# A hybrid SSD + HGRN2 + PEER block on one Trainium2 core: the sequence goes through the mixers in two token halves, and all dense gates are scattered instead of built from one-hot products

## The chip, the cores and the metric

The kernel runs on one core of one Trainium2 chip. The metric is device time in microseconds (us) of that core. A core has five engines that run their own instruction streams: TensorE (PE in the rows, with its weight loads as PEld), VectorE (DVE), ScalarE (ACT), GpSimd (POOL) and SyncE (SP), which only issues transfers here. Everything is in fp32.

## The reference

One encoder block on 1024 tokens of width 1024:

```python
hn   = rmsnorm(x, ln_mix_w)
z, xbc, dt_raw, q, f, i, g = split(hn @ w_in)          # 7184 columns
y_ssd = ssd_mixer(z, xbc, dt_raw, ...)                 # Mamba-2: 16 heads in 4 groups, state 128
y_hg  = hgrn2_mixer(q, f, i, g, lb, hg_norm_w)         # 8 heads, keys and values 128
h = x + concat(y_ssd, y_hg) @ w_out
xn = rmsnorm(h, ln_ffn_w)                              # PEER: 8 product-key heads
s  = (xn @ w_query) . sub_keys                         # 2 x 128 scores per head and token
expert, gate = top 16 of the 16 x 16 best pairs, softmax
y  = sum_k gelu(xn . u_table[expert_k]) * gate_k * v_table[expert_k]
out = rmsnorm(h + y, ln_final_w)                       # 16384 experts, 128 picks per token
```

Both mixers are recurrences over the sequence: the state after one chunk of tokens enters the next.

## The kernel before, in words

Tokens are cut into 8 blocks (chunks) of 128; a half is 4 of them. The program is a row of stages, each in a block of its own, at whose end every engine waits for all others.

1. `input_norm` normalises and turns x.
2. `ssd` goes over 4 groups, and in each over both halves. PE projects ("pieces") the next group-half while it runs the 4 chunks of this one; the first group-half is projected ahead of the first chunk. POOL makes one `ssd_awide` for each chunk. The last 8 chunks carry the pieces of HGRN2's head 0.
3. `hgrn` goes over 8 heads of 8 chunks. 56 chunks carry the pieces of the next head, the last 8 ("deep") have none. On DVE, `attend` forms each chunk's attention: seven strided products of the level scores with a mask (L1057), one more (L1059), and a sum over the levels (L1063). ACT starts two transfers that zero the part of the table `sel` that belongs to one pair of blocks.
4. `mix_out` multiplies by w_out, adds x, normalises (block by block), and runs 16 of the 32 query and score steps. A step gives the scores of two units; a unit is one head for one block of 128 tokens. DVE routes 32 of the 64 units here: MAX8, FIND_INDEX8 and MATCH_REPLACE8 of both key lists (L1176 to L1189), 54 candidate pairs, `route_hit` (L1219, L1221), its sum (L1223), indices and gate. POOL first scales Y (L1595), then scatters the gates of block 0 into `sel` in DRAM: 8 units of 16 indirect transfers each (L1604).
5. `peer`: blocks 0 to 3 are dense (every expert's row is multiplied, and the gates are read from `sel`); blocks 4 to 7 are gathered (the rows of the picked experts are fetched). For dense blocks 1 to 3 the gate table is first built: DVE makes one-hot rows (L2156, L2160), PE multiplies them (L1939), ACT copies them out and they are stored to `sel`. 96 such rounds stand ahead of the main loop.
6. The main loop goes over 16 groups of 8 first-keys: PE forms u products (L1958) and then v products (L1971), 256 slots in all, with 13 query steps (L1888, L1903) between. POOL gathers 512 rows of u and 512 of v, each of 128x1024; DVE multiplies and adds them (L2185, L2196), and routes the last 31 units.

The order on each engine is written out by hand in the code; semaphores join the engines.

Of the kernel before, what the change touches and what calls it, by code (L numbers as in the profile page):

```python
# [9 lines left out]
U32 = mybir.dt.uint32  # L10

P = 128
SEQ, D = 1024, 1024
NB = SEQ // P
KT = D // P
# [7 lines left out]
TAPS = 4  # L23
SSD_COLS = CT * P + XW + HPG
# [11 lines left out]
HEAD_PARTS = [[0], [1], [2, 3], [4, 5]]  # L36
LEVELS = 7
# [10 lines left out]
DB = NB // 2  # L48
DU, GU = PH * DB, PH * (NB - DB)
UNITS = DU + GU  # L50
DS, STEPS = DU // 2, UNITS // 2
GE = 8
NG = KEYS // GE
SLOTS = 2 * GE
UT = 3
PAIRS = GU * TOPK // 2
ROWS = GU * TOPK
# [4 lines left out]
MB = DB - 1  # L62
PAIR = 2 * DB * P
# [8 lines left out]
class Own:  # L72
# [17 lines left out]
    def skip(self):  # L90
        self.eng.sem_inc(self.sem, 1)
        self.n += 1

# [12 lines left out]

def prime(eng, sems):
    for s in sems:
        eng.sem_inc(s, 1)


def constants(nc, pool, C, filled, cut, ident_ready):
# [10 lines left out]
    nc.gpsimd.memset(C["lmask"][:], 1.0).then_inc(filled, 1)  # L123
# [11 lines left out]
                            base=0, pattern=[[0, NB], [1, P]], channel_multiplier=0)  # L135
    n = 0
    for j in range(LEVELS):
# [3 lines left out]
        m = C["lmask"][:, j, :].rearrange("p (q two r) -> p q two r", two=2, r=h)  # L141
# [9 lines left out]
    nc.gpsimd.affine_select(out=C["lmask"][:, LEVELS, :], in_=C["lmask"][:, LEVELS, :],  # L151
                            compare_op=ALU.is_equal, fill=0.0,
                            base=0, pattern=[[-1, P]], channel_multiplier=1).then_inc(cut, 1)
    pool.wait_ge(cut, n + 1)


def input_norm(nc, x, ln_w, w_ssd, C, hnT, w_group, group_in):


    with ExitStack() as ctx:  # L160
# [12 lines left out]

        xs = sb("xs", [P, NB, D])
# [16 lines left out]
        def _(sp):  # L191
# [5 lines left out]
            for i, part in enumerate(SSD_PARTS):  # L197
                sp.dma_start(w_group[:, :, part], w_ssd[0, :, :, part]).then_inc(group_in[i], 16)

        @block.gpsimd  # L200
        def _(pool):
            constants(nc, pool, C, filled, cut, ident_ready)
# [46 lines left out]
def first_weights(Y, kt):  # L249

    return Y[:, kt // 2, D + kt % 2 * HG_COLS:D + (kt % 2 + 1) * HG_COLS]


def first_piece(Y, half, p):

    if p < 2:
        return Y[:, KT // 2 + p, D + half * HALF:D + (half + 1) * HALF]
    return Y[:, KT // 2 + 2 + half, D + (p - 2) * 2 * P:D + (p - 1) * 2 * P]


def first_raw(Y, half):

    vg = Y[:, KT // 2 + 2 + half, D:MIX].rearrange("p (c x) -> p c x", x=2 * P)
    return first_piece(Y, half, 0), first_piece(Y, half, 1), vg[:, :, P:2 * P], vg[:, :, 0:P]


class Heads:
# [3 lines left out]
    def __init__(self, nc, ctx, first, hw):  # L271
# [12 lines left out]
        flat = first.rearrange("p k c -> p (k c)")  # L284
        self.first = flat
        self.w = hw[:, 0:KT * HG_COLS].rearrange("p (k c) -> p k c", k=KT)
# [3 lines left out]
        self.v = [sb("v0", [P, HC, P])]  # L290
        self.gs = [sb("gs0", [P, HC, P])]
        self.gend = sb("gend", [P, NB])
        self.G, self.k, self.q, self.ke, self.qs = [[flat[:, i * HALF:(i + 1) * HALF]] for i in range(5)]
        self.W = [flat[:, 5 * HALF:(5 + LEVELS) * HALF].rearrange("p (j l) -> p j l", j=LEVELS)]
        self.w_in, self.lb_in = [plain_sem(f"w_in{i}") for i in range(len(HG_PARTS))], plain_sem("lb_in")
        self.lb_diff, self.lb_ready = sem("lb_diff"), sem("lb_ready")
# [6 lines left out]
    def second(self, nc, ctx):  # L303
        def sb(name, shape):
            return ctx.enter_context(nc.sbuf_tensor("head_" + name, shape, F32))
# [11 lines left out]
def heads_act(nc, act, H, n, half, part, raw):  # L317

    raw_q, raw_f, raw_g = raw
    G, W = H.G[half], H.W[half]  # L320
    if part == 0:
        nc.scalar.activation(G, raw_f, ACT.Sigmoid).then_inc(H.gate_sig, 1)
        nc.scalar.activation(H.q[half], raw_q, ACT.Silu).then_inc(H.q_ready, 1)
# [15 lines left out]
def heads_dve(nc, dve, prep, H, u, half, part, reset, raw_v):  # L339
# [41 lines left out]
    else:  # L381
# [4 lines left out]
        prep.check()  # L386


def ssd(nc, w, w_in, w_ssd, par, w_hg, lb_logits, C, hnT, Y, spent, hw, H):

# [1955 lines left out]
```

## Time and profile before

| | |
|---|---|
| median of 3 runs | 3615.16 us (3612.87 to 3615.65) |
| span of the profiled execution | 3610.9 us, 4.3 under the median |
| PE busy | 3447.2 us, 95% of the span |
| DVE busy | 2815.0 us, 78% |
| POOL busy | 1422.8 us, 39% |
| ACT busy | 1079.8 us, 30% |
| granted TensorE clock, mean | 0.981 of full speed |

The profiled execution has no time of its own apart from its span, which counts from the first to the last instruction; what lies around the span is taken as the 4.3 us between it and the median. A high busy share says that the engine has work in most of the span. It doesn't say which engine ends a given stage.

### The profile page before, as it was taken

How to read it: one execution, taken by the hardware profiler on the slowest of the kernel's cores; microseconds unless marked ns; L12 is line 12 of the kernel's file. 1: busy time of each engine (PE TensorE's matmuls, PEld its weight loads, DVE VectorE, ACT ScalarE, POOL GpSimd, SP SyncE). 2: the span in 40 equal slices, each digit the busy share in tenths (PEclk: the TensorE clock that was granted, in tenths of full speed). 3: DMA queues.
4: the chain of work that ended last, by engine and by line, in shares of the span. 5: the costliest groups of instructions: out<-in, count | busy, mean ns of one | idle time of the engine just before them, and what ended most of it. 6: DMA issues, size and time to landing. Idle time of an engine off the chain costs nothing.

```text
span 3610.9 us, 39997 instructions
## 1 busy us (share of the span) xinstructions
PE 3447.2 (95%) x11593; PEld 1976.1 (55%) x11593; DVE 2815.0 (78%) x6484; ACT 1079.8 (30%) x2721; POOL 1422.8 (39%) x1233
## 2 busy tenths in 40 slices
PE   7999999999997999768799999999999999999998
PEld 4666666777774566556344444444444444444443
DVE  2466686776774389899788888987898889888898
ACT  3233344544442222268221112111211121121212
POOL 1000000000001277500566565655666566655665
PEclk9999999999997999989899999999999999999999
DMA  3111013000002234247999999999999999999998
GB/s 112 30 36 35 0 32 109 23 23 29 29 35 114 50 60 91 34 139 203 394 393 377 393 380 392 379 380 356 394 372 387 386 397 377 375 394 377 390 376 340
DMA packets 313936, 829.65 MB, mean 230 GB/s; under 512 B 41504, under 2 KB 145056, under 8 KB 305056
## 3 DMA queue, kind: packets, MB, share of 16 engines
q0 software_dynamic: 165888, 537.01, 39.9%
q1 hardware_dynamic: 125104, 227.45, 17.4%
q10 hardware_dynamic: 22768, 63.18, 4.5%
q8 instruction: 69, 1.13, 0.1%
q14 instruction: 107, 0.88, 0.1%
HBM read 789.73 MB, written 37.81 MB: 229 GB/s over the span
## 4 chain that ended last, share of the span: by engine, by line
PE 46%; issue 5%; DVE 3%; DMA 2%; POOL 1%; ACT 0%; ACTq 0%; DVEq 0%; POOLq 0%
PE peer_ps_o L1971 23%; PE peer_ps_d L1958 20%; PE peer_ps_q L1888 2%; DMA peer_vr<-in_v_rows,peer_index 2%; DVE Y L2196 1%; POOL peer_vr L1863 0%; DVE peer_mt L2156 0%; DVE peer_mt L2160 0%; POOL peer_ur L1856 0%; DVE peer_ur L2185 0%; PE peer_ps_s L1903 0%; DMA peer_ur<-in_u_rows,peer_index 0%; DVE route_hit L1221 0%; DVE peer_chosen L1223 0%; DVE Y L2213 0%
## 5 line engine op out<-in xcount | busy, mean ns | idle before, releaser
L1856 POOL DMA_INDIRECT peer_ur<-in_u_rows,peer_index x512 | 566.1, 1106 | 600.1 <-DVE peer_ur L2185 418.7
L2196 DVE SCALAR_TENSOR_TENSOR Y<-peer_vr,osq,Y 128x1024 f32<-128x1024 f32 x512 | 656.7, 1283 | 100.2 <-DMA peer_vr<-in_v_rows,peer_index 99.8
L1863 POOL DMA_INDIRECT peer_vr<-in_v_rows,peer_index x512 | 588.3, 1149 | 324.9 <-issue 148.2
L2185 DVE SCALAR_TENSOR_TENSOR peer_ur<-peer_ur,Y 128x1024 f32<-128x1024 f32 x512 | 627.6, 1226 | 8.0 <-DMA peer_ur<-in_u_rows,peer_index 8.0
L1958 PE MATMUL peer_ps_d<-hnT,route_ut 128*128 128x512 f32 x1376 | 598.6, 592 | 0.7 <-ACT peer_vr L2031 0.7
L1971 PE MATMUL peer_ps_o<-hw,Y 128*128 128x512 f32 x1024 | 446.2, 595 | 14.8 <-DVE Y L2172 14.7
L1971 PE MATMUL peer_ps_o<-hnT,Y 128*128 128x512 f32 x1024 | 442.6, 592 | 0.0
L1958 PEld LDWEIGHTS peer_ps_d<-hnT,route_ut 128*128 128x128 f32 x1376 | 261.2, 190 | 328.6 <-issue 327.7
L1971 PEld LDWEIGHTS peer_ps_o<-hw,Y 128*128 128x128 f32 x1024 | 194.9, 191 | 257.5 <-issue 235.9
L1971 PEld LDWEIGHTS peer_ps_o<-hnT,Y 128*128 128x128 f32 x1024 | 193.5, 190 | 238.2 <-issue 238.0
L1958 PE MATMUL peer_ps_d<-hnT,peer_ut 128*128 128x512 f32 x672 | 297.3, 595 | 6.7 <-ACT Y L2039 6.7
L2046 ACT ACTIVATE osq<-osq 128x2 f32<-128x2 f32 x256 | 51.2, 200 | 786.5 <-DVE peer_ur L2185 786.4
L2039 ACT ACTIVATE Y<-peer_ps_d 128x512 f32<-128x512 f32 x128 | 76.4, 597 | 672.9 <-PE peer_ps_d L1958 672.9
L1604 POOL DMA_INDIRECT sel<-route_ut,mo_sel_index x128 | 208.2, 1626 | 151.0 <-DVE route_ut L1247 83.1
L512 PE MATMUL ssd_ps_piece<-hnT,w_group 128*128 128x512 f32 x512 | 229.8, 602 | 6.9 <-ACT hw L595 5.1
L1589 POOL IOTA mo_count_u<- 128x128 uint32 x1 | 0.2, 239 | 590.6 <-POOLq L816 590.6
L1958 PEld LDWEIGHTS peer_ps_d<-hnT,peer_ut 128*128 128x128 f32 x672 | 128.2, 191 | 168.0 <-issue 168.0
L494 POOL TENSOR_TENSOR ssd_awide<-ssd_a,tri 128x512 f32<-128x512 f32 x32 | 34.5, 1078 | 453.3 <-PE ssd_ps_rows L556 404.5
L905 PE MATMUL hg_ps_piece<-hnT,hw 128*128 128x512 f32 x448 | 198.7, 597 | 4.3 <-ACTq L1027 4.3
L909 PE MATMUL hg_ps_piece<-hw,hnT 128*128 128x256 f32 x896 | 198.0, 379 | 0.0
L909 PEld LDWEIGHTS hg_ps_piece<-hw,hnT 128*128 128x128 f32 x896 | 168.1, 190 | 21.7
L512 PEld LDWEIGHTS ssd_ps_piece<-hnT,w_group 128*128 128x128 f32 x512 | 98.8, 193 | 129.6 <-issue 123.7
(331 smaller groups left out, 5018.8 us busy)
## 6 DMA issues: line engine op xcount, KB each, us to landing
route_ut<-in_u_cols SPq DMA_DIRECT2D x86, 512.0 KB, 7.4
hw<-in_v_cols SPq DMA_DIRECT2D x16, 2048.0 KB, 11.0
peer_mt<-sel ACTq DMA_DIRECT2D x64, 512.0 KB, 9.2
hnT<-in_v_cols SPq DMA_DIRECT2D x16, 2048.0 KB, 13.6
peer_ut<-in_u_cols SPq DMA_DIRECT2D x42, 512.0 KB, 7.3
route_wk<-in_w_route ACTq DMA_DIRECT2D x14, 1024.0 KB, 7.8
hnT<-in_w_route SPq DMA_DIRECT2D x9, 1024.0 KB, 4.8
route_wk<-in_w_route SPq DMA_DIRECT2D x9, 1024.0 KB, 6.9
```

Of the source, the lines that this page charges most:

```text
L512: mm = nc.tensor.matmul(bank, w[:, k, i * P:(i + 1) * P], hnT[:, half, k, :], start=(k == 0), stop=(k == KT - 1))
L905: mm = nc.tensor.matmul(bank, w[:, kt, p * P:(p + 1) * P], hnT[:, half, kt, :], start=(kt == 0), stop=(kt == KT - 1))
L909: mm = nc.tensor.matmul(bank[:, 0:2 * P], hnT[:, half, kt, cols(p - 2)], w[:, kt, 2 * P:4 * P], start=(kt == 0), stop=(kt == KT - 1))
L1604: pool.indirect_dma_start(sel.rearrange("a i q two (t o) -> (a i q two t) o", o=1), bass.IndirectOffsetOnAxis(ap=sel_index[:, h, k:k + 1], ...
L1856: pool.indirect_dma_start(ur[:, r % RING, :], None, u_rows, bass.IndirectOffsetOnAxis(ap=index[:, r // TOPK % 4, r % TOPK:r % TOPK + 1], a ...
L1863: pool.indirect_dma_start(vr[:, r % RING, :], None, v_rows, bass.IndirectOffsetOnAxis(ap=index[:, r // TOPK % 4, r % TOPK:r % TOPK + 1], a ...
L1888: mm = nc.tensor.matmul(ps_q[:, p, :], wq[:, k, p * P:(p + 1) * P], xg[:, k, :], start=(k == 0), stop=(k == KT - 1))
L1958: mm = nc.tensor.matmul(ps_d[:, e % 2, :], ut[e % UT][:, k, :], xT[:, k, :], start=(k == 0), stop=(k == KT - 1))
L1971: mm = nc.tensor.matmul(ps_o[:, o % OB, :], ht(e, tb), v_tile(e, half), start=(j == 0), stop=(j == GE - 1))
L2039: nc.scalar.activation(ht(e), ps_d[:, e % 2, :], ACT.Gelu).then_inc(gelu_done, 1)
L2185: nc.vector.scalar_tensor_tensor(out=ur[:, s, :], in0=ur[:, s, :], scalar=1.0, in1=Y[:, b, D:MIX], op0=ALU.mult, op1=ALU.mult, accum_out=d ...
L2196: nc.vector.scalar_tensor_tensor(out=hb, in0=vr[:, s, :], scalar=hid[:, c:c + 1], in1=hb, op0=ALU.mult, op1=ALU.add).then_inc(comb_done, 1)
```

## The change

The three stages ssd, hgrn and mix_out now run for tokens 0 to 511 and then again for tokens 512 to 1023; peer follows. SSD states, HGRN2 states (`held`) and the convolution's last columns (`carry`) are kept in SBUF between the halves. The weights of the mixers and w_out are loaded once in each half. Each half does two heads' first pieces in its ssd stage (`EARLY_HEADS`), so a half's hgrn stage has 24 chunks with pieces and 8 without.

All 32 dense units (`DENSE`) have their gates scattered to `sel`, 512 scatters in place of 128. The one-hot rounds, with their products, copies and stores, are gone. `sel` is zeroed as a whole (32 MB in 16 transfers, one for each chunk of the first ssd stage). Units 0 to 21 are routed in the first mix_out, 22 to 27 at the start of the second ssd stage, 28 to 31 within its first 8 chunks, 32 to 43 in the second mix_out, 44 to 63 in peer, which has 10 query steps in its loop. `attend` is now eight predicated copies, each after the one before (the next waits for it), with no sum; the mask is one of bytes.

```diff
+EARLY_HEADS = 2
+ROUTED_IN = [range(0, 22), range(UNITS // 2, 2 * ROUTED_STEPS)]
+ROUTE_BEFORE, ROUTE_AFTER, ROUTE_CHUNKS = range(22, 26), range(26, 28), range(28, 32)
+SCATTER_MIX0, SCATTER_PROLOGUE, SCATTER_SSD = DENSE[0:6], DENSE[6:9], DENSE[9:14]
+SCATTER_CHUNK = 5
+SCATTER_HG, SCATTER_MIX1 = DENSE[14:25], DENSE[25:]
...
+def scatter(nc, pool, R, sel, n, ks):
+    b, h, at = unit_block(n), unit_head(n), DENSE.index(n)
+    for k in ks:
+        if k == 0:
+            pool.wait_ge(R.routed, n + 1)
+            pool.wait_ge(R.gated, n + 1)
+            need(pool, R.scattered[b], 16 * TOPK * h)
+        nc.gpsimd.indirect_dma_start(sel..., IndirectOffsetOnAxis(ap=R.index_d[:, at, k:k + 1], axis=0),
+                                     R.gates_d[:, at, k:k + 1], None,
+                                     compute_op=ALU.add).then_inc(R.scattered[b], 16)
...
# ssd, GpSimd
+                for n in SCATTER_PROLOGUE:
+                    scatter(nc, pool, R, sel, n, range(TOPK))
...
                     nc.gpsimd.tensor_tensor(awide[:], ...)
+                    if half == 1:
+                        at = (t - first * HC) * SCATTER_CHUNK
+                        for q in range(at, min(at + SCATTER_CHUNK, len(SCATTER_SSD) * TOPK)):
+                            scatter(nc, pool, R, sel, SCATTER_SSD[q // TOPK], range(q % TOPK, q % TOPK + 1))
...
# hgrn, GpSimd
+            if half == 1:
+                for n in SCATTER_HG:
+                    scatter(nc, pool, R, sel, n, range(TOPK))
...
# hgrn, VectorE
-                    nc.vector.tensor_tensor(right(masked[:]), bank[:, j, 0:P // 2].rearrange(...),
-                                            right(C["lmask"][:]), ALU.mult)
-                nc.vector.tensor_tensor(masked[:, LEVELS, :], bank[:, LEVELS, :], C["lmask"][:, LEVELS, :],
-                                        ALU.mult).then_inc(mask_done, 1)
-                dve.wait_ge(mask_done, past(u * NB + c + 1))
-                nc.vector.tensor_reduce((att2 if lag and c % 2 else att)[:], masked[:].rearrange("p j l -> p l j"), AX.X,
-                                        ALU.add).then_inc(att_ready, 1)
+                    nc.vector.copy_predicated(right(to[:]), right(C["lmask"][:, j, :]),
+                                              bank[:, j, 0:P // 2].rearrange(...)).then_inc(G.placed, 1)
+                    dve.wait_ge(G.placed, past(t * LEVELS + j + 1))
+                nc.vector.copy_predicated(to[:], C["lmask"][:, LEVELS, :], bank[:, LEVELS, :]).then_inc(G.att_ready, 1)
...
# mix_out, GpSimd
-            for h in range(PH):
-                pool.wait_ge(R.routed, 2 * h + 1)
-                for k in range(TOPK):
-                    pool.indirect_dma_start(...).then_inc(R.scattered, 16)
+            for n in (SCATTER_MIX0, SCATTER_MIX1)[half]:
+                scatter(nc, pool, R, sel, n, range(TOPK))
...
# peer, VectorE and TensorE: the rounds ahead of the main loop
-                nc.vector.tensor_tensor(hot_a[j % 2], R.count[:]..., pickedT[:, b % 2, 0, t:t + 4]..., ALU.is_equal)
-                    ins = nc.vector.tensor_scalar(hot_b[j % 2][:, q, :], R.count[:], ..., ALU.is_equal, ALU.mult)
-                    mm = nc.tensor.matmul(ps_o[:, j % 2, q * P:(q + 1) * P], hot_a[j % 2][:, q, :], hot_b[j % 2][:, q, :])
```

**POOL.** Before, GpSimd has one awide for each of 32 chunks, nothing from there to mix_out but a memset, and its 128 scatters in mix_out (`Y<-Y,osq` is the scaling; `peer_ur` and `peer_vr` are the first gathers of the main loop):

```order
L494 TENSOR_TENSOR ssd_awide<-ssd_a,tri 128x512
L892 MEMSET hg_zero 128x256
L1595 TENSOR_TENSOR Y<-Y,osq 128x1024 x8
L1604 DMA sel<-route_ut,mo_sel_index 8388608x1 x128
L1856 DMA peer_ur<-in_u_rows,peer_index 128x1024 x5
L1863 DMA peer_vr<-in_v_rows,peer_index 128x1024 x5
```

In the changed kernel, from the first mix_out to the start of peer, the same engine has this:

```order
L1403 DMA sel<-lists 8388608x1 x96
L1403 DMA sel<-lists 8388608x1 x48
L559 TENSOR_TENSOR ssd_awide<-ssd_a,tri 128x512
L1403 DMA sel<-lists 8388608x1 x5
...
L1403 DMA sel<-lists 8388608x1 x176
L1770 TENSOR_TENSOR Y<-Y,osq 128x1024 x4
L1403 DMA sel<-lists 8388608x1 x112
L1969 DMA peer_ur<-in_u_rows,index_g 128x1024 x5
L1977 DMA peer_vr<-in_v_rows,index_g 128x1024 x5
```

96 scatters stand in the first mix_out, 48 ahead of the second ssd stage's first awide, 5 behind each of its 16 awides, 176 in the second hgrn stage, which had no GpSimd work before, and 112 in the second mix_out, ahead of all gathers.

**DVE, attend.** Before, VectorE has for each HGRN2 chunk (first rows of the stage's body):

```order
L1057 TENSOR_TENSOR hg_masked<-hg_ps_att,lmask 128x64
L1057 TENSOR_TENSOR hg_masked<-hg_ps_att,lmask 128x2x32
L1057 TENSOR_TENSOR hg_masked<-hg_ps_att,lmask 128x4x16
...
L1059 TENSOR_TENSOR hg_masked<-hg_ps_att,lmask 128x128
L1063 TENSOR_REDUCE hg_att<-hg_masked 128x128
```

and in the changed kernel:

```order
L1162 COPY_PREDICATED hg_att<-lmask,hg_ps_att 128x64
L1162 COPY_PREDICATED hg_att<-lmask,hg_ps_att 128x2x32
L1162 COPY_PREDICATED hg_att<-lmask,hg_ps_att 128x4x16
...
L1166 COPY_PREDICATED hg_att<-lmask,hg_ps_att 128x128
L404 TENSOR_SCALAR head_G<-head_G,head_oml,head_lb 128x512
```

Eight instructions stand for nine, and the copies write the attention tile itself.

**DVE, a chunk of the second ssd stage.** In each of its first 8 chunks half a unit's routing now stands between the preparation of the next group (`ssd_step`) and the update of the state, which before followed it directly:

```order
L788 TENSOR_SCALAR ssd_step<-ssd_step 128x16
L1315 MAX route_ti<-Y 128x8 x2
L1318 MAX_INDEX route_ix<-route_ti,Y 128x8
...
L1353 MAX route_best<-route_cand 128x8
L1355 MAX_INDEX route_place<-route_best,route_cand 128x8
L896 TENSOR_TENSOR state<-state,ssd_decay_all 128x256
```

## Rows read from the trace of the kernel before

**Rows 1.** Windows: length, busy us of each engine, PEclk, DMA share, GB/s.

```profile
28.20:121.70 93.50, 88.40 (x261) 50.66 (x261) 13.16 (x26) 15.63 (x28) 1.14 (x2) 0.95 0.15 46
121.70:446.90 325.20, 325.20 (x1235) 208.44 (x1235) 214.68 (x507) 121.80 (x202) 24.96 (x24) 1.00 0.08 23
446.90:538.90 92.00, 84.23 (x365) 59.47 (x364) 75.19 (x184) 39.42 (x66) 8.75 (x8) 0.99 0.08 24
538.90:1129.90 591.00, 564.14 (x2816) 430.59 (x2816) 437.37 (x1243) 268.10 (x570) 0.44 (x3) 0.96 0.12 39
1129.90:1219.60 89.70, 83.34 (x254) 43.70 (x255) 7.99 (x17) 18.93 (x61) 14.87 (x8) 0.96 0.32 128
1219.60:1547.00 327.40, 297.00 (x1115) 193.93 (x1113) 275.84 (x1140) 85.16 (x247) 208.17 (x128) 0.96 0.32 61
1547.00:1703.50 156.50, 125.82 (x849) 107.63 (x850) 147.66 (x429) 135.13 (x395) 5.25 (x5) 0.96 0.60 177
1703.50:3611.00 1907.50, 1868.72 (x4640) 872.10 (x4640) 1636.90 (x2930) 374.11 (x1117) 1149.10 (x1019) 0.99 0.98 381
```

**Rows 2.** Timeline of PE, ssd: start, us, line, [idle before].

```profile
135.31 0.38 PE L553 MATMUL ssd_ps_cb<-ssd_xc 128*128 128x128 f32 x2
...
148.85 0.38 PE L553 MATMUL ssd_ps_cb<-ssd_xc 128*128 128x128 f32 x2
```

**Rows 3.** Timeline of PE, hgrn: its start and two chunks.

```profile
547.17 8.81 PE L905 MATMUL hg_ps_piece<-hnT,hw 128*128 128x512 f32 x16 [4.30 <-ACTq L1027]
...
565.91 1.68 PE L926 MATMUL hg_ps_att<-w_group 128*128 128x64 f32 x14
...
575.39 1.67 PE L926 MATMUL hg_ps_att<-w_group 128*128 128x64 f32 x14
```

**Rows 4.** Timeline of DVE, one attend in hgrn.

```profile
1078.63 1.01 DVE L1057 TENSOR_TENSOR hg_masked<-hg_ps_att,lmask 128x64 f32<-128x64 f32 x7 [0.70 <-PE hg_ps_turn L928]
...
1079.87 1.92 DVE L1063 TENSOR_REDUCE hg_att<-hg_masked 128x128 f32<-128x1024 f32 x1
```

**Rows 5.** Groups of POOL: busy, mean ns, idle before by releaser.

```profile
L1863 POOL DMA_INDIRECT peer_vr<-in_v_rows,peer_index x512 | 588.3, 1149 | 324.9 <-issue 148.2 <-DMA sel<-peer_vr 117.2 <-DVE Y L2196 59.6
...
L1604 POOL DMA_INDIRECT sel<-route_ut,mo_sel_index x128 | 208.2, 1626 | 151.0 <-DVE route_ut L1247 83.1 <-issue 45.9 <-DMA sel<-route_ut,mo_sel_index 22.0
...
L1595 POOL TENSOR_TENSOR Y<-Y,osq 128x1024 f32<-128x1024 f32 x8 | 14.9, 1897 | 7.4 <-DVE osq L1644 7.4
...
L1589 POOL IOTA mo_count_u<- 128x128 uint32 x1 | 0.2, 239 | 590.6 <-POOLq L816 590.6
```

**Rows 6.** The scatters by source: ns min/median/max, first and last start.

```profile
L1604 POOL DMA_INDIRECT sel<-route_ut,mo_sel_index x128: 1542/1543/2417, 1234.9 to 1509.4; - x128
```

**Rows 7.** Timeline of POOL, two scatters in a row.

```profile
1240.73 1.54 POOL L1604 DMA_INDIRECT sel<-route_ut,mo_sel_index  x1 [0.30 <-issue]
...
1242.58 1.54 POOL L1604 DMA_INDIRECT sel<-route_ut,mo_sel_index  x1 [0.30 <-issue]
```

**Rows 8.** Timeline of DVE, mix_out: block 2's h, then units.

```profile
1245.70 1.22 DVE L1659 TENSOR_TENSOR Y<-mo_ps_h,hnT 128x1024 f32<-128x1024 f32 x1 [6.53 <-PE mo_ps_h L1405]
...
1251.63 0.48 DVE L1176 MAX8 route_ti<-route_sc 128x8 f32<-128x128 f32 x2
...
1260.99 0.48 DVE L1176 MAX8 route_ti<-route_sc 128x8 f32<-128x128 f32 x2
```

**Rows 9.** The chain that ended last, peer: start, us, engine, tile.

```profile
1786.75 23.13 PE peer_ps_o L1971 x50
...
1838.24 54.93 PE peer_ps_d L1958 x128
...
2363.84 6.91 PE peer_ps_q L1888 x32
...
2489.24 6.91 PE peer_ps_q L1888 x32
```

**Rows 10.** DMA issues of the span to 1140: KB, us to landing.

```profile
w_group<-in_w_ssd SPq DMA_DIRECT2D x16, 512.0 KB, 4.1
```

More of the change, by code:

```diff
@@ new lines, in _ @@
+            for n in (first, first + 1):
+                for p in range(SSD_PIECES):
+                    piece(n, p)
+            sums(first)
+            for n in range(first, end):
+                for c in range(HC):
+                    t, at = n * HC + c, cols(spot(n, c))
+                    if c == 0:
+                        pe.wait_ge(S.activated, past((n + 1) * CT))
+                    pe.wait_ge(S.wide_ready, past(t + 1))
+                    pe.wait_ge(S.att_ready, past(t))
+                    nc.tensor.matmul(ps_cb[:, 0:P], xc[:, 2, at], xc[:, 3, at], start=True, stop=True)
@@ new lines, in _ @@
+            if half == 1:
+                for i in range(2):
+                    sp.dma_start(ut[i], u_cols[i]).then_inc(R.u_in[i], 16)
+            load_x(first + 2)
+            load_queries(step + 2)
+            load_keys(step + 2)
+            load_queries(step + 3)
+            load_x(first + 3)
+            load_keys(step + 3)
+            loads(step + 4)
+            key_loads(step + 4)
+            loads(step + 5)
+            key_loads(step + 5)
+            for i in TAIL:
+                load_queries(i)
+                load_keys(i)
@@ L1523, in root @@
             def root(b):
-                act.wait_ge(h_meaned, past(b + 1))
-                nc.scalar.activation(rs[:, b:b + 1], ss[:, b:b + 1], ACT.Sqrt).then_inc(h_rooted, 1)
-            for b in range(NB):
-                now, late = HEADS_IN[b], late_head(b - 1)
-                if b == FIRST:
+                act.wait_ge(M.h_meaned, past(b + 1))
+                nc.scalar.activation(rs[:, b:b + 1], ss[:, b:b + 1], ACT.Sqrt).then_inc(M.h_rooted, 1)
+            unit = 2 * step
+            out_y(first, EARLY)
@@ L1542, in _ @@
                     out_y(b + 1, LATE)
-                    query_out(now[2])
-                    gates(2 * now[1])
+                    query_out(step + 2)
+                    gates(unit + 2)
                     continue
-                if late is not None:
-                    score_out(late)
-                    gates(2 * late - 1)
-                if b == NB - 1:
-                    for g in range(DB, DB + 2):
-                        x_copy(g, 0)
-                        x_copy(g, 1)
@@ L1584, in _ @@
-            gates(DU - 1)
-            score_out(DS)
+                if at == HC - 1:
+                    score_out(step + 3)
+                    query_out(step + 4)
+                    gates(unit + 6)
+                root(b)
+                if at == HC - 1:
+                    gates(unit + 7)
+                    score_out(step + 4)
+                    query_out(step + 5)
+            done = unit + 8
+            for i in TAIL:
+                if i == PH:
+                    x_copy(end - 1, 0)
+                    x_copy(end - 1, 1)
+                query_out(i)
+                score_out(i - 1)
+                if i > TAIL[0]:
+                    gates(done)
+                    done += 1
@@ L1685, in peer @@
+                if at == FIRST:
+                    for n in range(unit + 2, unit + 6):
+                        route(n)
+            routed = unit + len(ROUTED_IN[half])
+            for n in range(unit + 8, routed):
+                route(n)
+            for n in range(routed - GATE_LAG, routed):
+                route_gates(nc, dve, R, n)
+def peer(nc, w_route, u_cols, v_cols, u_rows, v_rows, fin_w, sel, C, Y, osq, hw, hnT, R, ut, out):
     with ExitStack() as ctx:
@@ L2291, in laid_out @@
+        peer(nc, w_route, u_cols, v_cols, u_rows, v_rows, fin_w, sel, C, Y, osq, hw, hnT, R, ut, out)
 def laid_out(inputs):
```

1981 lines of the change are left out of this document (953 added, 1028 removed).

## Prediction

> **What bounds the kernel now.** I read first where time goes by stage. A window for each stage [rows 1] gives 93.5 us (first projection of ssd), 325.2 (24 ssd chunks with pieces), 92.0 (the last 8), 591.0 (hgrn), 89.7 and 327.4 (mix_out up to and from the first routed unit), 156.5 (the one-hot rounds) and 1907.5 (the main loop). In each the reader should set PE's busy time against the length: 325.2 of 325.2, 564 of 591, 1869 of 1908, but only 297 of 327.4 in the routed part of mix_out (DVE 275.8) and 126 of 156.5 in the rounds (DVE 147.7). So PE bounds ssd, hgrn and peer; mix_out and the rounds are shared with DVE.
>
> Then the period of each repeated piece. An ssd chunk with pieces takes 148.85 − 135.31 = 13.54 us [rows 2], an hgrn chunk with pieces 575.39 − 565.91 = 9.47 [rows 3]. In peer's chain, the query steps at 1893.17 (1838.24 + 54.93) and 2363.84 are four groups apart, 117.67 each; a group without a query step has 110.7 (6.91 less) [rows 9].
>
> Last the engine that the change loads, POOL. It idles 590.6 us until the end of hgrn [rows 5]: nothing crosses a stage's end, so its scatters can't run ahead into another stage. A scatter takes at least 1.54 us of POOL [rows 6], and two undisturbed ones start 1.85 apart [rows 7]. Over all 128 the busy time is 208.2 and the issue gaps 45.9, 1.985 each, and 22.0 went into landing waits [rows 5].
>
> **The price of a unit of scatters.** Floor 16 × 1.85 = 29.5 us; the mean of before 16 × 1.985 = 31.8; with the landing waits 34.5 ((208.2 + 45.9 + 22.0)/8). The landing wait is for the head before of the same block; the changed order alternates two blocks, so a whole unit lies between, and I drop it. The long scatters of before (up to 2.42 us [rows 6]) fall in stretches of routing on DVE. In the second hgrn stage DVE does no routing, so I take 30.8, between floor and mean.
>
> The Trainium skill, "SBUF — State Buffer", section "Who interferes with whom", says that copies, casts and tensor_scalar on VectorE can hold a port pair that GpSimd needs to write descriptors, while tensor_tensor and tensor_reduce don't hold descriptor writing up. The spread of 1.54 to 2.42 us agrees, but doesn't single out which instruction did it. By that rule the hgrn stage, with few such instructions, would run near the floor, 29.5 a unit, and the whole sum below would come out 14 us lower for the 11 units of that stage.
>
> **The sum by stages**, from the span's 28.2 us where input_norm ends.
>
> *First ssd half.* 93.5 + 8 chunks with ssd pieces (8 × 13.54 = 108.3) + 92 = 293.8: ends at 322. The zeroing of 32 MB adds 2 MB a chunk, 5.5 us of 13.54 at peer's 381 GB/s, where the DMA share is 0.08 [rows 1]: hidden; if it is not, weights come late by some us a group.
>
> *First hgrn half.* Of the 56 chunks with pieces it has 24, and all of the last 8: 591 − 32 × 9.47 = 288. The start's 4.3 us wait [rows 3] goes, since the second head's pieces are made ahead; 1.5 for the stage's end. attend took 1.24 for its eight products and 1.92 for the sum [rows 4], 3.2. Eight predicated copies cost at least 1.2 (no dearer than the products), and, each waiting for the one before, at most 8 × 0.48 = 3.8 (a short dependent DVE step, MAX8's row [rows 8], is the nearest). I take 2.6. It counts only in the 8 chunks without pieces, elsewhere PE's 9.47 covers it: −4, ends −16 to +5. So 281 (269 to 290): ends at 603.
>
> *First mix_out half.* 89.7 to the first unit; then 22 units on DVE. A unit is 1260.99 − 1251.63 = 9.36 [rows 8], with its gate 9.7: 213.6. Blocks 2 and 3's h stand between: 6.53 idle and 5.93 from h to the next unit [rows 8] for the first, some 19 for both. 322.5; the 6 scattered units (185 us) fit beside. Ends at 925.5. DVE sets this stage: PE has about half of mix_out's 380 us.
>
> *Second ssd half.* 293.8 again, plus: the first weights are loaded inside the stage, 4.1 us [rows 10], I take 4.5; the gates of 4 units and their waits ahead of the first chunk, 4; three units (48 scatters, 92 us) ahead of the first awide are just done when it is wanted, 3. Four units' routing (39 us) goes into the first 8 chunks. DVE idles (325.2 − 214.7)/24 = 4.6 us a chunk, 37 in eight [rows 1], but in pieces, and half a unit is 5.5 in one chunk and 3.8 in the next: between 8 and 20 us late, I take 13. Five scatters a chunk (9.6) fit in 13.54. 318.5: ends at 1244.
>
> *Second hgrn half.* PE's path is 281 as before. POOL has 11 units: 11 × 30.8 = 339 (325 to 350). It starts them at the stage's start, the last lands before no one may leave: 340.5, ends near 1584. This is the term that decides: 59 us of waiting for POOL.
>
> *Second mix_out half.* DVE: 89.7 + 12 × 9.7 + 15 = 221. POOL scales 4 blocks (7.4 idle, then 4 × 1.86 [rows 1, 5]: 14.9), then 7 units, 215.6: 230 and 1.5 for the end. POOL ends it too: 1815.5, which I round down to 1814.5, since its start waits are partly DVE's.
>
> *peer.* No rounds, no stores to `sel` that v gathers wait for (117.2 us of POOL's waits [rows 5], before the loop's steady part). From the first u product to the first v product it took 1786.75 − 1703.50 = 83.3 [rows 1, 9]. Now there is a query step as well (6.9) and no store: at least 54.9 + 6.9 = 62, at most 90; I take 73, for the first u rows and routes must still come. Then 55.8 (2 × 27.47 + 0.89, the chain's 1838.24 − 1786.75 is 51.5 for what was left of it), 15 groups, 9 of them with a query step: 9 × 117.67 + 6 × 110.76 = 1723.6. The end: 3610.9 less 1838.24 less 13 × 117.67, 2 × 110.76 and the one long group's 7.7 (2363.84 to 2489.24 is 125.4) leaves 13.8. 1866, against 1907.5. Ends at 3681.
>
> With the 4.3 us between the span and the median: **3685 us**, +1.9%. Against before by parts: ssd +102, hgrn −29, mix_out +127, rounds −156.5, peer −41, together +2; POOL's hold +59 and +9. The DVE routing that filled time in mix_out beside 8 blocks' products now has only half of them to hide behind, and that eats the rounds' gain; POOL then decides the sign.
>
> **The rivals.**
>
> *Scatters at their floor and cheap attends.* 11 × 29.5 = 325 and 7 × 29.5 = 206.5: −14 and −9; attends at 1.2 take another 10 in the first hgrn half. 3652, up to 3668. For it: two scatters in a row show 1.85 [rows 7]. Chance 0.2.
>
> *Dearer scatters.* At 34.5 a unit (each waits for a landing, or DVE disturbs it) hgrn has 380 and mix_out 242 + 15: +40 and +26. With the ssd stage's routing at its upper end, 3715 to 3755. For it: the rate of before, taken whole. Against: the order of blocks. Chance 0.12.
>
> *POOL is off the path (no change).* Were the scatters to overlap, or an hgrn stage as long as POOL's by another cause, the sum without POOL's hold is 3617, against 3615.2. It needs a unit under 281/11 = 25.5 us, 1.6 us a scatter, which would have to be less than busy time and gap together show (1.85). Chance 0.07.
>
> *Faster.* POOL's hold must be gone (as above), or the rest must be 75 us better: mix_out's first half is the place. If DVE's units there don't wait for the start of 89.7 and take 1 us less each than I reckon (22 us), and peer starts in 62 rather than 73, and the copies are at 1.2, the sum falls by 22 + 11 + 12 = 45 and POOL's hold grows by nothing: 3640, still slower. It decides only with scatters below 27 us a unit as well (11 × 3.8 = 42 less): 3600. Chance 0.1.
>
> **How the numbers follow.** Forecast (POOL holds the second hgrn and mix_out stages, 3668 to 3715) 0.51, floor 0.2, dearer 0.12, no change 0.07, faster 0.1. The range leaves out the faster and no-change cases and the upper part of the dearer one, and reaches down into the floor case: 3640 to 3725. A measurement of this kernel can tell about 0.2% (7 us) from no change. Faster 0.1, same 0.07, slower 0.83.
>
> **What would show it.** In the second hgrn stage PE would have some 60 us idle at the end, with POOL's 176 scatters end to end at 1.92 us; the stage 340 us against 281 of the first. In the first mix_out DVE near 90% busy from its first unit to its end, PE about 60%. In the second ssd stage chunks of 14 to 16 us in the first eight and 13.5 in the first half's. In peer the period stays 117.67 and its length is about 1866. It would be wrong if scatters run under 27 us a unit, if chunks of hgrn stay PE-bound but take longer (copies dearer than 3.8), if the routing in ssd costs more than 20 us, or if peer's gathers, now free of the stores, shorten its groups below PE's 110.7, which PE's work rules out.

## The result

The changed kernel takes 3754.69 us (median of 4 runs, 3748.37 to 3756.04) against 3615.35 us: a ratio of 1.0386, 95% interval 1.0371 to 1.0400. It is slower by 139 us. The forecast was 3685 with a range up to 3725; the sign was right, the size was not.

The span of the profiled execution is 3754.3 us. PE is busy 3378 us of it (90%, before 95%), DVE 2654 (71%), POOL 2062 (55%, before 39%). The windows of the changed kernel by stage, in the columns of [rows 1]: first ssd, first hgrn, first mix_out, second ssd, second hgrn until PE's last product, from there to the stage's end, second mix_out, peer.

```profile
28.20:314.70 286.50, 278.12 (x1024) 177.34 (x1024) 155.11 (x373) 96.69 (x163) 18.90 (x19) 0.99 0.45 161
314.70:597.20 282.50, 259.62 (x1312) 200.31 (x1312) 184.60 (x595) 126.75 (x268) 0.02 (x1) 0.94 0.18 58
597.20:926.00 328.80, 253.58 (x992) 174.16 (x992) 210.16 (x907) 62.52 (x188) 165.26 (x102) 0.88 0.35 85
926.00:1230.50 304.50, 283.90 (x1024) 180.94 (x1024) 249.01 (x769) 99.45 (x190) 224.59 (x144) 0.96 0.36 57
1230.50:1510.20 279.70, 258.77 (x1312) 199.74 (x1312) 181.04 (x575) 126.76 (x266) 233.12 (x139) 0.95 0.37 54
1510.20:1578.80 68.60, 0.00 (x0) 0.00 (x0) 1.10 (x3) 0.37 (x2) 57.25 (x37) 0.51 0.22 0
1578.80:1818.70 239.90, 170.90 (x576) 101.25 (x576) 112.12 (x452) 44.25 (x134) 188.92 (x116) 0.86 0.37 72
1818.70:3754.30 1935.60, 1863.59 (x4512) 857.92 (x4512) 1554.19 (x2536) 335.43 (x1054) 1163.32 (x1024) 0.98 0.97 373
```

Two windows speak. In the sixth PE has no product for 68.6 us while POOL alone works: that is the forecast hold of the second hgrn stage. The last one is the surprise. Peer starts at 1818.7, where the sum had it at 1814.5, and then takes 1935.6 us, where the sum had 1866 and the kernel before 1907.5. The whole miss, 70 us, lies in peer. (The 4 us by which peer starts late are set off by what lies around the span: the forecast took 4.3 us, and here it is 3756.04 − 3754.3 = 1.7.)

The timelines of the changed kernel at the hold (PE, then POOL's last scatters of the stage):

```profile
1509.81 0.39 PE L1059 MATMUL hg_ps_o<-head_v,hg_att 128*128 128x128 f32 x2
1582.32 1.94 PE L1555 MATMUL mo_ps_y<-ident,Y 128*128 128x128 f32 x8 [72.12 <-DVEq L1795]
...
1575.14 1.55 POOL L1403 DMA_INDIRECT sel<-lists  x1 [0.30 <-issue]
1576.99 1.55 POOL L1403 DMA_INDIRECT sel<-lists  x1 [0.30 <-issue]
```

PE's last product of the stage starts at 1509.8, the last scatter ends at 1578.5, and the next stage's first product comes at 1582.3. The wait is put down to a sequencer, not to POOL, since it is the barrier at the stage's end that releases PE; the engine that came last has to be looked up in its own timeline.

In peer's chain before, one group with a query step came every 117.67 us [rows 9]. The chain of the changed kernel (in each row: start, us, engine, tile, line):

```profile
2196.52 6.91 PE peer_ps_q L2002 x32
...
2322.45 6.91 PE peer_ps_q L2002 x32
...
2371.87 20.07 DMA peer_vr<-in_v_rows,index_g
2391.97 1.28 DVE Y L2200
2393.25 0.98 DVE lists L1360
...
2395.34 1.06 DVE route_chosen L1364
2397.59 51.45 PE peer_ps_o L2052 x114
...
3077.95 20.61 PE peer_ps_d L2039 x48
...
3192.84 54.93 PE peer_ps_d L2039 x128
3247.78 54.93 PE peer_ps_o L2052 x128
3302.71 54.93 PE peer_ps_d L2039 x128
```

Query step to query step is 125.9 us here, and from the first step (1823.78) to the eleventh group (3077.95) ten groups take 1254.2, 125.4 each. The late groups, which have neither query nor routing, run in 109.87, PE's own work. The eleventh, which still has routing but no query step, takes 3192.84 − 3077.95 = 114.89. From the second to the eleventh group the chain leaves PE: the last gathered v row takes 20 us to land in the group shown (17 to 22 in the others), VectorE waits for it, finishes its routing and the last masked product, and only then PE starts its v products (L2052). The same place in PE's timeline:

```profile
2378.16 7.03 PE L2039 MATMUL peer_ps_d<-hnT,state 128*128 128x512 f32 x16
2385.02 6.17 PE L2052 MATMUL peer_ps_o<-hw,Y 128*128 128x512 f32 x14
2397.59 2.93 PE L2052 MATMUL peer_ps_o<-hw,Y 128*128 128x512 f32 x3 [6.39 <-DVE Y L2176]
```

PE makes the v products of seven of the group's eight keys and then waits 6.39 us for VectorE's masked product of the eighth. In the whole of peer such waits come to 55.1 us on the page of the changed kernel, ten of them, one in each group from the second to the eleventh. On the page before they came to 14.7, and none of it lay in the thirteen groups with a query step:

```profile
L2052 PE MATMUL peer_ps_o<-hw,Y 128*128 128x512 f32 x1024 | 466.2, 615 | 55.1 <-DVE Y L2176 55.1
```

The first reason that offered itself: the change moved the query steps (`next_query`) from the second half of a group, where PE makes v products, into the first, and with them the 1 MB weight load on ScalarE's queue.

```diff
-            i = DS + (m + 3) // 2
-            return i if m % 2 == 1 and i < STEPS else None
+            i = first_step + m // 2
+            return i if m % 2 == 0 and i < STEPS else None
```

(`m` counts half-groups.) The diff shows it in one line; the front part of this document did not quote it, and the prediction did not read it.

### The profile page after: what moved, and what is told of

Same layout as the page of the kernel before. It is cut to its first block, busy times and chain, and to the rows that moved or that the text cites. A ratio compares the mean times of both kernels' runs of the same rounds, so it can differ in the third digit from the quotient of the medians.

```text
span 3754.3 us, 36373 instructions
## 1 busy us (share of the span) xinstructions
PE 3378.3 (90%) x10816; PEld 1900.1 (51%) x10816; DVE 2653.5 (71%) x6220; ACT 913.5 (24%) x2301; POOL 2061.6 (55%) x1618
## 4 chain that ended last, share of the span: by engine, by line
PE 39%; DMA 5%; DVE 4%; issue 2%; POOL 1%; ACT 0%; DVEq 0%; ACTq 0%; POOLq 0%
PE peer_ps_o L2052 22%; PE peer_ps_d L2039 15%; DMA peer_vr<-in_v_rows,index_g 5%; PE peer_ps_q L2002 2%; DVE Y L2200 1%; DVE peer_ur L2189 1%; POOL peer_ur L1969 0%; DVE lists L1362 0%; DVE route_chosen L1364 0%; DVE lists L1360 0%; POOL peer_vr L1977 0%; DVE Y L2176 0%; DMA wk<-in_w_route 0%; DVE route_ix L1326 0%; DVE route_ix L1318 0%
## 5 line engine op out<-in xcount | busy, mean ns | idle before, releaser
L1403 POOL DMA_INDIRECT sel<-lists x512 | 836.8, 1634 | 292.9 <-issue 151.9
L1969 POOL DMA_INDIRECT peer_ur<-in_u_rows,index_g x512 | 564.1, 1102 | 523.6 <-DVE peer_ur L2189 396.4
L1977 POOL DMA_INDIRECT peer_vr<-in_v_rows,index_g x512 | 599.2, 1170 | 235.1 <-issue 146.0
L2052 PE MATMUL peer_ps_o<-hw,Y 128*128 128x512 f32 x1024 | 466.2, 615 | 55.1 <-DVE Y L2176 55.1
L2052 PE MATMUL peer_ps_o<-hnT,Y 128*128 128x512 f32 x1024 | 442.7, 592 | 0.0
L2052 PEld LDWEIGHTS peer_ps_o<-hw,Y 128*128 128x128 f32 x1024 | 201.1, 198 | 315.6 <-issue 249.5
L2052 PEld LDWEIGHTS peer_ps_o<-hnT,Y 128*128 128x128 f32 x1024 | 194.4, 190 | 243.9 <-issue 243.5
L2039 PE MATMUL peer_ps_d<-hnT,held 128*128 128x512 f32 x688 | 302.3, 592 | 0.0
L2039 PE MATMUL peer_ps_d<-hnT,state 128*128 128x512 f32 x688 | 302.3, 592 | 0.0
L2039 PEld LDWEIGHTS peer_ps_d<-hnT,state 128*128 128x128 f32 x688 | 130.5, 190 | 161.4 <-issue 161.2
L2039 PEld LDWEIGHTS peer_ps_d<-hnT,held 128*128 128x128 f32 x688 | 130.4, 190 | 161.4 <-issue 161.2
L2176 DVE TENSOR_TENSOR Y<-Y,peer_mt 128x512 f32<-128x512 f32 x128 | 88.5, 691 | 153.4 <-ACT Y L2082 152.5
L1024 PE MATMUL hg_ps_piece<-hnT,hw 128*128 128x512 f32 x384 | 172.4, 602 | 0.3 <-DMA hw<-in_w_hg 0.3
```

Source lines behind the costliest of these rows:

```text
L1024: mm = nc.tensor.matmul(bank, w[:, kt, p * P:(p + 1) * P], hnT[:, half, kt, :], start=(kt == 0), stop=(kt == KT - 1))
L1403: nc.gpsimd.indirect_dma_start(sel.rearrange("a i q two (t o) -> (a i q two t) o", o=1), bass.IndirectOffsetOnAxis(ap=R.index_d[:, at, k:k ...
L1969: nc.gpsimd.indirect_dma_start(ur[:, r % RING, :], None, u_rows, bass.IndirectOffsetOnAxis(ap=R.index_g[:, r // TOPK % RQ, r % TOPK:r % TO ...
L1977: nc.gpsimd.indirect_dma_start(vr[:, r % RING, :], None, v_rows, bass.IndirectOffsetOnAxis(ap=R.index_g[:, r // TOPK % RQ, r % TOPK:r % TO ...
L2039: mm = nc.tensor.matmul(ps_d[:, e % 2, 0:DT], ut[e % UT][:, k, :], xT[:, k, 0:DT], start=(k == 0), stop=(k == KT - 1))
L2052: mm = nc.tensor.matmul(ps_o[:, o % OB, :], ht(e, tb), v_tile(e, side), start=(j == 0), stop=(j == GE - 1))
```

## The experiments

**The place of the query step and of its load.** Two runs move them apart. In the first only the load is issued 8 slots later:

```diff
-                if i is not None and sl == 6:
+                if next_query(m - 1) is not None and sl == 6:
+                    i = next_query(m - 1)
                     if i + 1 < STEPS:
                         load_query(i + 1)
```

> The changed kernel, with one transfer moved: in peer, the load of the next query step's weights (1 MB and 128 KB, on ScalarE's queue) is issued 8 slots later, in the half of a group in which PE makes v products, as it was before the change; the query steps themselves stay where the change put them. Theory 1 (the load meets the 2 MB v load, the u loads and the gathers in the first half, a gathered v row then lands 18 to 20 us after its issue, VectorE waits, and PE waits 4 to 6 us at the first v product of each group): the ten groups go from 125.4 us back to about 118, and the whole falls by 60 to 77 us, to about 3685. Theory 2 (it is the query step in the first half that upsets the order of work between PE, ACT and VectorE, whatever the load does): less than 15 us of it comes back.

Measured: 3722.50 us, ratio 1.0299 (1.0282 to 1.0316). 32 us come back: neither theory. In PE's timeline of this run the wait at the first v products is shorter but still there in each of these groups, and in three groups PE also waits 0.5 to 2.7 us for the weights at the query step itself:

```profile
2260.13 23.42 PE L2052 MATMUL peer_ps_o<-hw,Y 128*128 128x512 f32 x50 [2.81 <-DVE Y L2177]
2311.53 7.17 PE L2002 MATMUL peer_ps_q<-xg,wk 128*128 128x256 f32 x32 [0.52 <-DMA wk<-in_w_route]
2383.14 23.42 PE L2052 MATMUL peer_ps_o<-hw,Y 128*128 128x512 f32 x50 [2.60 <-DVE Y L2177]
```

In the second, step and load both go where they were before:

```diff
-            return i if m % 2 == 0 and i < STEPS else None
+            return i if m % 2 == 1 and i < STEPS else None
...
-            n = 2 * first_step - 1 + m
-            return n if m >= 1 and n < UNITS else None
+            n = 2 * first_step - 2 + m
+            return n if m >= 2 and n < UNITS else None
```

> The changed kernel, with peer's ten query steps (and so their weight loads) in the second half of each group, where the kernel before had them, and the routing of the units of peer one half-group later. Theory 1 and theory 2 both expect 60 to 77 us back (about 3685). A third theory (the groups are longer because of the routing of units on VectorE or because sel is read where it was scattered, not because of queries or their loads) expects them to stay at 125 us, and the whole within 10 us of 3754.

Measured: 3682.44 us, ratio 1.0196 (1.0179 to 1.0213). 72 us come back, so the third theory is out: the routing moved a half-group later too, but each half-group still routes one unit. The 72 are somewhat too many for peer. Of the 74 us between the two spans, 6 lie in PE's wait at the end of the second hgrn stage (66.0 us in this run, 72.1 in the changed kernel), which the edit doesn't touch; and the kernel before took 3611.9 us beside this run and 3615.4 beside the changed one. Some 68 us are peer's. Its chain has the period of before again (2114.75, 2232.41, 2350.08: 117.67). What it looks like at the first v product, PE first, then VectorE:

```profile
2343.05 7.03 PE L2039 MATMUL peer_ps_d<-hnT,state 128*128 128x512 f32 x16
2349.92 7.07 PE L2002 MATMUL peer_ps_q<-xg,wk 128*128 128x256 f32 x32
2356.82 27.63 PE L2052 MATMUL peer_ps_o<-hw,Y 128*128 128x512 f32 x64
...
2345.75 1.29 DVE L2200 SCALAR_TENSOR_TENSOR Y<-peer_vr,osq,Y 128x1024 f32<-128x1024 f32 x1 [3.94 <-DMA peer_vr<-in_v_rows,index_g]
...
2353.36 1.29 DVE L2200 SCALAR_TENSOR_TENSOR Y<-peer_vr,osq,Y 128x1024 f32<-128x1024 f32 x1 [2.21 <-DMA peer_vr<-in_v_rows,index_g]
...
2358.25 0.68 DVE L2176 TENSOR_TENSOR Y<-Y,peer_mt 128x512 f32<-128x512 f32 x1
```

VectorE still waits for v rows (3.94 and 2.21 us), and its last masked product comes only at 2358.25. But PE has no idle time: it makes the query step just then.

The eleventh group of this run has routing but no query step, and there the wait is back:

```profile
3065.41 24.46 PE L2052 MATMUL peer_ps_o<-hw,Y 128*128 128x512 f32 x50 [3.32 <-DVE Y L2176]
```

It takes 3117.34 − 3001.15 = 116.2 us in the chain, against 117.67 for the groups with a query step. In this place a step of 6.91 us lengthens a group by only 1.5 (up to 2.8 in the other runs that have it there).

That gave a fourth theory: a query step is worth its place between the last u product and the first v product, where it fills a wait. It is tested by putting the step (and load) into the same half, two slots later (`sl == 2` instead of `sl == 0`):

> The changed kernel with peer's query steps and their weight loads in the second half of each group, but two slots into it instead of just ahead of its first v product. Theory 4 (the query step is worth its place only just ahead of the first v product, where PE waits for VectorE's last masked product and the query's 6.9 us fill that wait; the load in the first half is a second, smaller loss): the stall at the first v product is back without the load's part, as in the run with the later load, 3715 to 3730. Rival (any place in the second half will do, since the first half is the one in which transfers are dense): 3680 to 3690, with no PE idle ahead of the first v products.

Measured: 3733.79 us, ratio 1.0339 (1.0321 to 1.0356), 4 us over the expectation, 44 over the rival's upper end and 51 over the run with the step ahead of the v products. The wait is back, with the step right behind it:

```profile
2370.39 6.17 PE L2052 MATMUL peer_ps_o<-hw,Y 128*128 128x512 f32 x14
2380.14 9.46 PE L2052 MATMUL peer_ps_o<-hw,Y 128*128 128x512 f32 x18 [3.58 <-DVE Y L2176]
2389.44 7.07 PE L2002 MATMUL peer_ps_q<-xg,wk 128*128 128x256 f32 x32
```

So the place just ahead of the v products decides, not the half: routing and half are those of the run before, and only the slots within the half differ. The fourth pair of places was to show whether load and step add (the load in the first half, the step ahead of the v products):

> The changed kernel with peer's query steps just ahead of the first v product of each group (3682), but the weight load of the next one in the first half of the group, where the change has it. It is the fourth of the four pairs of places of step and load (first half and first half 3755, step first and load second 3722, step ahead of v and load second 3682). If the step fills PE's wait for VectorE up to its own 6.9 us, most of the load's delay is covered: 3685 to 3700. Rival (the load costs its 32 us wherever the step stands): 3710 to 3720.

Measured: 3731.15 us, ratio 1.0327 (1.0312 to 1.0343). Both expectations miss, and the trace shows why this run can't answer the question: the load is now issued so shortly before its own step that PE waits for it (chain of this run).

```profile
2242.28 8.72 DMA wk<-in_w_route
2251.04 7.17 PE peer_ps_q L2002 x32
```

PE waits 2.66 us there in this group, and 2.7 to 3.6 in the others. I had counted slots, not the 9 us from issue to landing against them. How much of the load's 32 us is hidden behind a well-placed step stays open.

**GpSimd's hold.** The second hgrn stage without its 176 scatters:

```diff
+    if n in SKIPPED:      # SKIPPED = set(SCATTER_HG)
+        return
```

> The changed kernel without the 176 scatters (11 units) of the second hgrn stage; the gates of these units are missing from the dense part, so this leaves out part of the result. The waits for landed scatters count the fewer ones. If GpSimd alone holds that stage: PE's last product there ends 275 us after the stage's start, and the stage falls from 348 to about 278, 66 to 71 us less in all, about 3686. Rival (something else on the path, another queue or VectorE, ends the stage shortly after PE's work): less than 40 us.

Measured: 3681.57 us, ratio 1.0185 (1.0163 to 1.0207): 73 us less (part of the result is left out). PE's last product starts at 1506.1 and the next stage's first at 1508.5, so nothing else stood behind the scatters. The length of the hold differs between executions: in the runs that keep all 176 scatters there, PE's wait is 64 to 72 us (64.1 with the step two slots later, 72.1 in the changed kernel).

> The edits of the last two together: query steps in the second half of a group, and no scatters in the second hgrn stage (part of the result is left out). If the two losses are apart from each other they add: 3754 less 70 less 69, about 3615, the time of the kernel before. Rival: peer's groups are slow for a reason that comes from GpSimd's backlog, and the gains don't add: over 3640.

Measured: 3616.26 us, ratio 1.0013 (1.0003 to 1.0023), 138 us less than the changed kernel, where 72 and 73 would add to 145. The two losses are nearly separate, and together they are as large as the 139 us between the kernels.

> The run with query steps ahead of the first v product (3682), without the 18 units of scatters of the second hgrn and second mix_out stages (their gates are missing from the result). GpSimd then holds neither stage: 70 us less in hgrn, and in mix_out 236 us become what VectorE's routing needs, about 221: 3595 to 3602, 10 to 17 us faster than the kernel before. Rival (VectorE's routes or PE need as long as GpSimd in mix_out): 3610 or more.

Measured: 3599.35 us, ratio 0.9964 (0.9950 to 0.9978). Without any hold of POOL after the second ssd stage the new order of stages is 13 us faster than before. That is all that the missing rounds, the halves and the copies bring, and 288 scatters, without which part of the result is missing, had to be free for it. Against the run before it 17 us are gained, 15 of them in PE's wait between the last product of the second mix_out and peer's first (52.3 and 37.1 us).

**Scatters placed otherwise.** With the query steps ahead of the v products, the gates of the first mix_out divided one unit after their routing instead of three (not shown here), and:

```diff
-SCATTER_MIX0, SCATTER_PROLOGUE, SCATTER_SSD = DENSE[0:6], DENSE[6:9], DENSE[9:14]
+SCATTER_MIX0, SCATTER_PROLOGUE, SCATTER_SSD = DENSE[0:7], DENSE[7:10], DENSE[10:16]
-SCATTER_HG, SCATTER_MIX1 = DENSE[14:25], DENSE[25:]
+SCATTER_HG, SCATTER_MIX1 = DENSE[16:25], DENSE[25:]
...
+                        at, count = (7 * i, 7) if i < 8 else (16 + 5 * i, 5)
```

> The run with query steps ahead of the first v product (3682), and GpSimd's scatters placed otherwise: the first mix_out's gates are divided on VectorE one unit after their routing instead of three, so that scatters start some 25 us earlier and 7 units go there instead of 6; 7 scatters in each of the first 8 chunks of the second ssd stage; 9 units instead of 11 in the second hgrn stage. If GpSimd's queue alone holds the second hgrn stage, that falls from 348 to about 283 us, and the fuller chunks cost up to 7: 3620 to 3632. Rival (scatters slow down in the fuller chunks, or the gates' earlier wait holds VectorE in mix_out): 3645 or more.

Measured: 3632.96 us, ratio 1.0054 (1.0038 to 1.0071), 1 us over the range. PE's wait at the end of the second hgrn stage, in this run's timeline:

```profile
1532.97 1.94 PE L1556 MATMUL mo_ps_y<-ident,Y 128*128 128x128 f32 x8 [16.68 <-DVEq L1799]
```

16.7 us are left of 72.1. The fuller chunks cost 6 us, at the upper end of what was expected: from the first to the last chunk start of the second ssd stage it is 201.8 us, against 195.7 in the changed kernel. The kernel is still 20 us slower than before.

**The predicated copies.** First the other way round, the changed kernel with products and a sum in its first hgrn half (in `attend`: `tensor_tensor` with the mask, `tensor_reduce` over the levels):

> The changed kernel, where the first hgrn half forms its attention as before the change, with eight products and a sum over the levels, in place of eight predicated copies (3.2 against 2.3 us on VectorE); the second half keeps the copies. The copies' gain counts only in the 8 chunks without pieces: 0.9 us each, so 4 to 8 us longer, 3758 to 3763. Rival (VectorE matters in all 32 chunks): 25 us or more longer.

Measured: 3759.46 us, ratio 1.0405 (1.0381 to 1.0428). It is 5 us more in the median, but the runs spread over 18 us (3750.33 to 3768.50), and in its trace the stage is 11.6 us longer (289.7 against 278.1 from PE's first product of it to the next stage's first). It excludes the rival, and the trace shows why: the chunks with pieces come every 9.43 to 9.48 us in both, and the difference lies in the last 8 chunks and the stage's start and end. It doesn't size the gain. The kernel before with the copies alone does:

```diff
-                    nc.vector.tensor_tensor(right(masked[:]), bank[:, j, 0:P // 2]..., right(C["lmask"][:]), ALU.mult)
+                    nc.vector.copy_predicated(right(to[:]), right(bytemask[:, j, :]), bank[:, j, 0:P // 2]...
+                                              ).then_inc(placed, 1)
+                    dve.wait_ge(placed, past((u * NB + c) * LEVELS + j + 1))
...
-                nc.vector.tensor_reduce((att2 if lag and c % 2 else att)[:], masked[:].rearrange("p j l -> p l j"), ...)
```

> The kernel before with one part of the change alone: the eight products and the sum of each HGRN2 attention are eight predicated copies there too (VectorE's instructions of that stage written out instead of looped). attend falls from 3.2 to 2.3 us on VectorE. It counts in the 8 chunks without pieces, where PE waits for VectorE: 4 to 8 us less than before, a ratio near 0.998. Rival (those chunks are held by PE, ScalarE or the preparation of heads): within 2 us of before.

Measured: 3607.89 us (median of 11 runs), ratio 0.9983 (0.9974 to 0.9992). The next stage's first product in the kernel before, and in this run:

```profile
1129.94 1.97 PE L1386 MATMUL mo_ps_y<-ident,Y 128*128 128x128 f32 x8 [2.49 <-SPq L1338]
...
1125.82 1.97 PE L1385 MATMUL mo_ps_y<-ident,Y 128*128 128x128 f32 x8 [2.50 <-SPq L1337]
```

The hgrn stage starts at 538.90 and 539.02, so 4.2 of the 6 us are seen in it. That VectorE's loop is also written out here is no rival: the chunks with pieces, which are the looped ones, keep their 9.43 to 9.48 us. This is the fastest version that keeps the whole computation: 6 us better than before, 147 better than the change.

## Why the prediction was wrong, step by step

**Up to peer the sum held.** First ssd and hgrn halves: 293.8 + 281 = 575 forecast, 597.2 − 28.2 = 569 measured. First mix_out 322.5, measured 328.8; from its first routed unit (687 us) on VectorE was busy in 84% of the time and PE in 71%, where I had named 90 and 60. Second ssd 318.5, measured 304.5: 98.4 up to the first chunk where I took 105, 117.7 for the first eight chunks where I took 121.3, 88.5 for the rest where I took 92. The 13 us for being late in its chunks held in size (the runs don't part the routing's share from that of the five scatters a chunk): from the first chunk's start to the sixteenth's it is 195.7 us (1024.37 to 1220.05), against 183.5 in the first half (119.93 to 303.44), 12.2 more. PE waits for VectorE there, most of all in the eighth chunk, which takes 19.6 us where I had named 14 to 16:

```profile
1138.86 0.83 PE L644 MATMUL ssd_ps_y<-state,ssd_xc 128*128 128x256 f32 x2 [4.43 <-DVE ssd_dec L869]
```

Second hgrn 340.5, measured 348.3. POOL issued the 176 scatters in 1578.54 − 1234.80 = 343.7 us, 31.2 a unit, where I took 30.8. Second mix_out 231.5, measured 239.9. Peer's start came 4 us late, with errors of both signs that cancel, which is luck in part. The term called deciding, POOL's hold of 59 us, measured 73 by leaving the scatters out.

**attend.** Forecast at 2.6 us, measured in the changed kernel's timeline:

```profile
542.62 1.94 DVE L1162 COPY_PREDICATED hg_att<-lmask,hg_ps_att 128x64 f32<-128x64 uint8 x7 [1.35 <-PE hg_ps_turn L1047]
544.60 0.30 DVE L1166 COPY_PREDICATED hg_att<-lmask,hg_ps_att 128x128 f32<-128x128 uint8 x1
```

2.28 us from the first start to the last end, against 3.16 in [rows 4]. It counts only in chunks without pieces, as said: the chunks with pieces have the same period with either form.

**The step that failed** is "15 groups, 9 of them with a query step: 9 × 117.67 + 6 × 110.76", and, in the list of what would be seen, "in peer the period stays 117.67". I took a group's price from a kernel in which the query step stood at one place and paid it for another place. With its first group and start counted, the sum gave the ten query groups 128.8 + 1059.0 = 1187.8 us (73, 55.8 and nine periods); they took 3077.95 − 1818.7 = 1259.2. These 71 us are the miss. The six groups behind them came out as forecast, 664.5 us against 6 × 110.76 = 664.6, but not because a group without a query step takes 6.91 less than one with it: the first of them, with routing, took 114.9, the others 109.9. None of the rivals had it: the only sentence on the length of groups argued that they can't get shorter than PE's work, and none asked whether they can get longer. The run that puts step and load back where they were gives 72 us back, and 65 on top of the missing scatters (3681.57 to 3616.26). What failed is thus the period taken for peer's groups: it left out a wait of PE for VectorE that the old place of the step had filled. The trace of before has the sign of it. Apart from the first, its fifteenth group is the only one with routing and no query step, and there PE waits at the same point:

```profile
3439.60 21.73 PE L1971 MATMUL peer_ps_o<-hw,Y 128*128 128x512 f32 x50 [3.02 <-DVE Y L2172]
```

**What a period is made of.** Of the 8 us that one of the nine later groups with a query step loses, 5.8 in the mean are idle (4.1 to 8.0) and the rest is a slower PE just behind. Windows of the changed kernel ahead of, in and behind the wait of the group shown above (the columns of [rows 1]; PEclk is the last but two):

```profile
2360.00:2385.00 25.00, 25.00 (x59) 11.02 (x58) 19.94 (x38) 7.05 (x18) 13.89 (x12) 1.00 1.01 407
2391.20:2397.60 6.40, 0.01 (x1) 0.01 (x1) 5.50 (x9) 0.00 (x0) 1.01 (x1) 0.82 1.03 409
2397.60:2403.00 5.40, 5.40 (x8) 2.32 (x9) 5.40 (x8) 0.68 (x3) 2.44 (x2) 0.58 1.01 397
2403.00:2410.00 7.00, 7.00 (x18) 3.17 (x17) 6.71 (x10) 0.68 (x3) 5.48 (x6) 1.00 0.96 353
```

The granted clock is 1.00 before the wait, 0.58 in the 5.4 us behind it (mostly the 1.2 GHz level), and 1.00 again after. In the chain above, the 114 v products behind the wait take 51.45 us; at the pace of the late groups (128 in 54.93) they would take 48.9. So the slow stretch costs 2.5 us in this group, on top of 6.4 idle.

**Right for the wrong amount**: the "dearer" rival (3715 to 3755) contains the measured time, but by another mechanism (34.5 us a unit), which did not happen. It is no credit.

**The reason of the change's loss, then**, as far as the runs show it: 73 us of POOL's hold in the second hgrn stage, some 70 us of query steps and their loads taken from the place where the steps filled a wait of PE, and 17 us of a second hold, mostly in mix_out (3616 against 3599). Without the three the new order of stages is 13 us faster than the old. The parts taken singly add to some 10 us more than the 139 measured; the first two overlap by 7. Of the second part, the load's place alone gives 32 us back when it is moved and the step's place the other 40; how the two share it in another order stays open, as said above.

## What to carry to other kernels

A period read from a trace belongs to the order in which its pieces stand: when a change moves a piece within a repeated body, look up what its old place covered, even if the piece's own duration is unchanged. Compare the index functions that place work (here one line in `next_query`), not only the loops that are added or removed. Work taken from engines with slack (a one-hot build beside other work) and given to a serial queue (here 512 scatters, 1.9 us apart) has to be summed over the stages between which that queue can't run ahead.

## What the runs showed of the hardware

In the second hgrn stage, which scatters took long was not what the prediction had taken. Between 1236 and 1500 us of the changed kernel's timelines there are 134 scatters; 19 took over 1.75 us, 97 under 1.60. Of the 19 long scatters 18 overlap a VectorE tensor_tensor on SBUF inputs (the products of L396 and L397 in runs above all), of the 97 short scatters 21 do. A copy, cast or tensor_scalar overlaps 1 of the 19 and 14 of the 97, a predicated copy 2 of 19 and 60 of 97. One of the slow ones (the two slowest took 3.65 us), and some of what VectorE did in it:

```profile
1263.29 1.70 POOL L1403 DMA_INDIRECT sel<-lists  x1 [0.31 <-issue]
1265.29 2.99 POOL L1403 DMA_INDIRECT sel<-lists  x1 [0.30 <-issue]
1268.58 1.55 POOL L1403 DMA_INDIRECT sel<-lists  x1 [0.30 <-issue]
...
1265.09 0.41 DVE L397 TENSOR_TENSOR head_W<-head_W,head_q 128x256 f32<-128x256 f32 x1
1265.43 0.42 DVE L396 TENSOR_TENSOR head_W<-head_W,head_k 128x256 f32<-128x256 f32 x1
```

The Trainium skill, "SBUF — State Buffer", section "Who interferes with whom", expects tensor_tensor not to hold up descriptor writing (it says so as inferred), while tensor_scalar and copies can; by that the stage should have run near 29.5 us a unit. It ran at 31.2, and the trace doesn't agree with that part of the rule. The same section also says, and the prediction left it out, that a VectorE instruction with two SBUF inputs contends with a GpSimd instruction that reads SBUF. The overlaps above fit that, if a scatter reads its indices and gates in this way; no run shows that it does. Overlap in a trace is no proof of a cause; no run here takes the tensor_tensors away.
